# Gate weights of four heads multiplied in pieces inside the delta-rule pairs

## The chip, the cores and the metric

One core of one Trainium2 chip runs the whole program in one launch. The metric is the device time of that execution in microseconds (us), the median of several runs. Engines are named as in the profile: PE (TensorE) with its weight loads PEld, DVE (VectorE), ACT (ScalarE), POOL (GpSimd), and SP, which issues the DMAs.

## The reference, cut to what matters

A step of a 4-layer decoder trunk on 256 prompt positions and 8 samples of 8 positions, 320 columns in all, model width 1024. Layer 3 mixes tokens with a gated DeltaNet of 8 heads of 128 channels. Everything is fp32.

```python
qkv = silu(causal_dwconv(h @ w_qkv, conv_buf, w_conv))     # q, k, v; width-4 convolution
ab = h @ w_ab                                              # beta and log decay g of each head
lmat = strict_lower((k * beta) @ k.T * decay)              # chunks of 64 positions
u, w = solve(lmat + I, [v * beta, k * beta * exp(gc)])     # unit lower triangular
for each chunk:                                            # the state S goes from chunk to chunk
    v_new = u - w @ S
    o = (q * exp(g)) @ S + (q @ k.T * decay) @ v_new
    S = S * exp(g_last) + (k * exp(g_last - g)).T @ v_new
gate = silu(h @ w_g)                                       # one [128 x 320] tile per head
y = (rmsnorm(o) * gate) @ w_out
```

## The kernel before

**Units.** A weight matrix streams in units of 128 x 1024 fp32 (512 KB). SP loads a unit into one of four slots `raw`, ACT copies it rounded to fp32r into `whi` (`split_hi`, L1427), POOL subtracts and leaves the rest in `wlo` (`split_lo`, L610 and L612, a half each), and PE multiplies it with 8 row tiles of the normalised input. Each row tile takes three matmuls of 320 columns (high times high, high times low, low times high: L893 to L895), so a unit is 24 matmuls into one PSUM bank. A slot is free again when PE is through with its unit.

**The value and gate stage** (`d_vg`) has 16 units, in turn one of values and one of a gate for each of the 8 heads. DVE evicts a value unit into a padded buffer (L2341, L2342) and runs the width-4 convolution over it (L2345, L2348), ACT applies silu (L1783, L1784) and keeps the tail (L1786). A gate unit takes one eviction (L2370) and one silu (L1793) into the tile `GT`. Between units the engines also work out beta, the decays and the norms (`ab_*` semaphores), which SP stores to memory and reads back as broadcast rows: `rows_in` counts the three loads of a head (L466 to L468).

**The pairs** (`gdn_pair`) then take the heads two by two, `x` = 0 and 1. Four banks belong to each head of a pair. A pair has these parts:

- start: DVE scales keys by their norm (`keys`, L2417), POOL by beta (`scaled_keys`, L676); PE multiplies keys by keys (L1251) and keys by queries (L1257); DVE makes the matrix to be inverted (L2466 to L2470); PE turns keys, values and that matrix (L1189). Three matmuls of ones, whose result nobody reads, follow (`idle`, L1234).
- five levels of a block inversion. In each, PE runs `below` for both heads (L1278), ACT copies the result (L1878), PE runs `change` (L1289; in the last level L1298), DVE subtracts and transposes (L2487, L2491; in the last level L2499). The order is fixed: below 0, below 1, change 0, change 1.
- chunk steps: four chunks, PE (L1333 to L1373) and DVE (L2514 to L2542) in turn. L1333 is the batch of samples, matmuls of 16 columns. Beside them ACT and POOL prepare the next pair (L1897, L1844, L1832; L676, L704, L706), and POOL decays the sample states (L712) and spreads values over samples (L719).
- end: two more matmuls of ones, the state updates of the samples (L1379, L1380), DVE's additions to the states (L2549, L2550) and the product with the gate (L2554).

Pair 0 is written out, pairs 1 and 2 (and on PE pair 3) come from a loop. Pair 3 splits units 2 and 3 of the output projection where the others prepare the next pair. The names `Hh_spare`, `Hl_spare`, `M`, `sd`, `fsil` are lent buffers. No scheduler moves instructions: each engine runs its own list in the order written, and semaphores join the lists.

## Time and profile before

| what | us |
|---|---|
| median of 3 runs | 1556.9 (1553.49 to 1559.3) |
| the profiled execution | 1555.36 |
| its span, first to last instruction | 1553.6 |
| PE matmul busy in the span | 1523.0 (98%) |
| PE weight loads busy | 1481.7 (95%) |
| DVE, ACT, POOL busy | 799.6, 734.0, 1076.1 |

The span is the profiled execution without 1.8 us around it. Busy times are sums over the whole program; the change touches only the stretch from the value and gate stage to the end of the pairs, some 230 us of it. Matmuls overlap one another and their ends are modelled, so the row PE is always fuller than the engine.

### The profile page before, as it was taken

What the parts mean: (1) busy time and instruction counts of PE and PEld (TensorE: products, weight loads), DVE (VectorE), ACT (ScalarE), POOL (GpSimd) and SP (SyncE); (2) the same over time, 40 slices, a digit from 0 to 9 for tenths busy, and PEclk for the clock granted to TensorE, in tenths of its full rate; (3) what the DMA queues carried; (4) which work ended last, traced back from release to release, by engine and by line L of the source; (5) the groups of instructions that cost most, each with busy time, mean ns of one, the idle gap of its engine ahead of it and who ended that gap; (6) DMA issues with size and microseconds to landing.
All of it is one profiled execution on the core that took longest, in us unless ns stands there. A gap on an engine that the chain in (4) does not pass through costs nothing.

```text
span 1553.6 us, 32327 instructions
## 1 busy us (share of the span) xinstructions
PE 1523.0 (98%) x10258; PEld 1481.7 (95%) x10258; DVE 799.6 (51%) x1791; ACT 734.0 (47%) x1406; POOL 1076.1 (69%) x1041
## 2 busy tenths in 40 slices
PE   9999999999999999999999999999899999999998
PEld 9999999998999999888999999999888889999997
DVE  4555544017455313996555521666668766555401
ACT  6654444445444435566544433557534424444432
POOL 5568887764777678986777767666655556767674
PEclk9999999999999999999999999999999989999999
DMA  6344444552444655312565445544412215444453
GB/s 240 122 139 149 151 148 154 148 148 93 152 156 141 163 147 167 106 58 89 166 158 162 138 138 142 186 134 138 135 62 77 77 63 183 153 158 141 124 150 112
DMA packets 88111, 212.49 MB, mean 137 GB/s; under 512 B 25601, under 2 KB 33313, under 8 KB 88033
## 3 DMA queue, kind: packets, MB, share of 16 engines
q1 hardware_dynamic: 88032, 211.49, 44.2%
q8 instruction: 43, 0.70, 0.2%
q14 instruction: 36, 0.29, 0.1%
HBM read 201.80 MB, written 9.66 MB: 136 GB/s over the span
## 4 chain that ended last, share of the span: by engine, by line
PE 91%; DVE 5%; ACT 1%; issue 1%; DMA 1%; DVEq 0%; SPq 0%; POOL 0%; ACTq 0%; POOLq 0%
PE bank L893 26%; PE bank L895 26%; PE bank L894 26%; PE bank L1131 2%; PE bank L1289 1%; PE bank L1278 1%; PE bank L1333 1%; PE bank L1363 1%; PE bank L1184 1%; DMA fst<-in_d_st 1%; PE bank L1351 1%; PE bank L1354 0%; DVE bank L2263 0%; DVE Hh_spare L2468 0%; PE bank L1315 0%
## 5 line engine op out<-in xcount | busy, mean ns | idle before, releaser
L610 POOL TENSOR_TENSOR wlo<-raw,whi 128x512 fp32r<-128x512 f32 (+3 forms) x398 | 458.5, 1152 | 376.1 <-ACT whi L1427 338.6
L893 PE MATMUL bank<-Gh,whi 128*128 128x320 f32 x1912 | 596.6, 312 | 3.1 <-DVE M L2245 1.9
L895 PE MATMUL bank<-Gh,wlo 128*128 128x320 f32 x1912 | 591.1, 309 | 0.0
L894 PE MATMUL bank<-Gl,whi 128*128 128x320 f32 x1912 | 590.8, 309 | 0.0
L612 POOL TENSOR_TENSOR wlo<-raw,whi 128x512 fp32r<-128x512 f32 (+3 forms) x398 | 479.2, 1204 | 0.0
L1427 ACT ACTIVATE whi<-raw 128x1024 fp32r<-128x1024 f32 (+3 forms) x400 | 374.9, 954 | 52.9 <-PE bank L895 38.2
L893 PEld LDWEIGHTS bank<-Gh,whi 128*128 128x128 f32 x1912 | 359.3, 188 | 5.4 <-DVE M L2245 2.2
L894 PEld LDWEIGHTS bank<-Gl,whi 128*128 128x128 f32 x1912 | 359.3, 188 | 1.1
L895 PEld LDWEIGHTS bank<-Gh,wlo 128*128 128x128 f32 x1912 | 359.0, 188 | 0.0
L893 PE MATMUL bank<-Hh,whi 128*128 128x320 f32 x912 | 284.1, 311 | 4.0 <-DVE Hl L2204 2.5
L895 PE MATMUL bank<-Hh,wlo 128*128 128x320 f32 x912 | 282.3, 310 | 0.0
L894 PE MATMUL bank<-Hl,whi 128*128 128x320 f32 x912 | 282.2, 309 | 0.0
L1496 ACT ACTIVATE bank<-bank,par 128x336 f32<-128x336 f32 x88 | 45.3, 515 | 309.2 <-DVE bank L1985 309.2
L893 PEld LDWEIGHTS bank<-Hh,whi 128*128 128x128 f32 x912 | 171.5, 188 | 5.6 <-issue 3.6
L894 PEld LDWEIGHTS bank<-Hl,whi 128*128 128x128 f32 x912 | 171.6, 188 | 0.1
L895 PEld LDWEIGHTS bank<-Hh,wlo 128*128 128x128 f32 x912 | 171.6, 188 | 0.0
L2019 DVE TENSOR_TENSOR X<-bank,X 128x320 f32<-128x320 f32 (+1 forms) x32 | 15.7, 492 | 245.7 <-PE bank L895 245.7
L1975 DVE TENSOR_TENSOR fpad<-bank,R 128x256 f32<-128x256 f32 x88 | 37.4, 425 | 179.8 <-PE bank L895 179.6
L1462 ACT ACTIVATE Gh<-X,par 128x320 fp32r<-128x320 f32 (+1 forms) x48 | 27.0, 563 | 115.2 <-DVE X L2019 77.2
L2010 DVE TENSOR_TENSOR tmp<-bank,R 128x320 f32<-128x320 f32 x88 | 43.3, 492 | 55.1 <-PE bank L895 55.1
L1980 DVE TENSOR_SCALAR bank<-fpad,par 128x336 f32<-128x336 f32 x88 | 50.2, 571 | 21.9 <-DVE fpad L1976 21.6
L1982 DVE SCALAR_TENSOR_TENSOR bank<-fpad,par,bank 128x336 f32<-128x336 f32 x88 | 50.4, 573 | 12.4 <-DVE bank L1980 11.6
(392 smaller groups left out, 1812.0 us busy)
## 6 DMA issues: line engine op xcount, KB each, us to landing
raw<-in_f_up SPq DMA_DIRECT2D x176, 512.0 KB, 3.4
raw<-in_f_down SPq DMA_DIRECT2D x64, 384.0 KB, 3.2
raw<-in_f_down SPq DMA_DIRECT2D x64, 320.0 KB, 3.2
raw<-in_c_pw SPq DMA_DIRECT2D x24, 512.0 KB, 3.6
raw<-in_a_in SPq DMA_DIRECT2D x16, 512.0 KB, 4.1
raw<-in_d_qk SPq DMA_DIRECT2D x16, 512.0 KB, 3.8
raw<-in_d_vg SPq DMA_DIRECT2D x16, 512.0 KB, 3.6
raw<-in_a_out SPq DMA_DIRECT2D x8, 512.0 KB, 3.6
```

Source lines behind the costliest of these rows:

```text
L610: pool.tensor_tensor(wlo[k][:, 0:half], raw[k][:, 0:half], whi[k][:, 0:half].bitcast(F32), ALU.subtract).then_inc(half_ready, 1)
L612: pool.tensor_tensor(wlo[k][:, half:w], raw[k][:, half:w], whi[k][:, half:w].bitcast(F32), ALU.subtract).then_inc(lo_ready, 1)
L893: nc.tensor.matmul(dst, wh, h, start=start and n == 0, stop=False)
L894: nc.tensor.matmul(dst, wh, lo, start=False, stop=False)
L895: ins = nc.tensor.matmul(dst, wl, h, start=False, stop=stop and end and n == len(tiles) - 1)
L1131: ins = nc.tensor.matmul(mixb[i][:, 0:NT], diag[i][:, n * P:(n + 1) * P], windows(i, CONVW - PETAPS[m] + n), start=n == 0, stop=n == PETAP ...
L1427: nc.scalar.activation(whi[k][:, 0:w], raw[k][:, 0:w], ACT.Copy).then_inc(hi_ready, 1)
L1496: nc.scalar.activation(mixb[i][:, 0:FW - 2], mixb[i][:, 0:FW - 2], ACT.Silu, bias=col("f", j * 4 + (l * FT * 4 + 3))).then_inc(sil_ready, 1)
L1975: S.mark(vec.tensor_tensor(fp[:, 2:at], prompt(acc[2 * i]), prompt(R), ALU.mult))
L1980: S.mark(vec.tensor_scalar(ft[:, 0:n], fp[:, 0:n], col("f", w), None, ALU.mult))
L1982: S.mark(vec.scalar_tensor_tensor(out=ft[:, 0:n], in0=fp[:, 1:n + 1], scalar=col("f", w + 1), in1=ft[:, 0:n], op0=ALU.mult, op1=ALU.add))
L2010: vec.tensor_tensor(tmp[i][:, :], acc[2 * i + 1][:, 0:NT], R[:, :], ALU.mult).then_inc(evac, 1)
```

## The change

The gate units of heads 1, 3, 5 and 7 leave the stage, which keeps 12 units (value, gate, value for each two heads). Pair b multiplies the gate unit of head 2b + 1 itself: its 24 matmuls go to bank 5 in pieces of 2 or 3 between the products of the levels. The unit sits in slot 1; SP loads it early, and in the chunk steps of the pair before ACT makes its high part (`gate_high`) and POOL its low part (`gate_low`, one instruction over 1024 columns). DVE evicts the gate after the last level (`late_evac`), ACT applies silu in the chunk steps. Both fillers `idle` go. The keys by queries of head x = 1 move behind its turned keys and values have been read, into bank 6. Pair 3 splits units 1, 2 and 3 of the output projection, where it split 2 and 3. The beta and decay steps of the stage move to earlier units (after units 4, 5, 9 and 10, before 5, 7 and 11). `vp`, the levels' masked matrices and the row differences move to other buffers, since the weight slots are now in use in the pairs.

```diff
-                             [("d_ab", 4, 2 * P), ("d_qk", 16, 8 * P), ("d_vg", 16, 8 * P),
+                             [("d_ab", 4, 2 * P), ("d_qk", 16, 8 * P), ("d_vg", 12, 8 * P),
@@ SP
+            def load_gate(b):
+                if isinstance(b, int):
+                    sp.wait_ge(half_ready, START["d_vg", 3] + 10)
+                    sp.wait_ge(lo_ready, START["d_vg", 3] + 10)
...
+                else:
+                    sp.wait_ge(late_lo, b)
...
+                sp.dma_start(raw[1][:, 0:UNIT], src).then_inc(late_in, 16)
@@ POOL
+            def gate_low(b):
+                pool.wait_ge(late_hi, b + 1)
+                pool.tensor_tensor(wlo[1][:, :], raw[1][:, :], whi[1][:, :].bitcast(F32), ALU.subtract).then_inc(late_lo, 1)
...
                         pool.wait_ge(qt_ready, h + 1)
                         pool.tensor_tensor(deci[x], mincl[:, 0:NT], ndif[x], ALU.subtract).then_inc(diffi_ready, 1)
+                    gate_low(b + 1)
@@ PE
+                    def gate(a, z):
+                        if a == 0:
+                            pe.wait_ge(late_hi, b + 1)
+                            pe.wait_ge(late_lo, b + 1)
+                        for i in range(a, z):
+                            kt, part = i // 3, i % 3
+                            w = (whi[1], whi[1], wlo[1])[part][:, kt * P:(kt + 1) * P]
+                            ins = nc.tensor.matmul(bank[5][:, 0:NT], w, tile_of((Gh, Gl, Gh)[part], kt),
+                                                   start=i == 0, stop=i == 3 * KT - 1)
...
+                        if x == 1:
+                            gate(0, 3)
                         pe.wait_ge(tt_ready, h + 1)
                         turn(bank[4 * x], TT[x]).then_inc(t_turned, 1)
-                    idle(3, bank[5][:, TW:512])
...
                         for x in range(2):
                             below(lev, x)
+                        gate(*((3, 5), (7, 9), (12, 14), (17, 19), (22, 24))[lev])
                         for x in range(2):
+                            if lev == 0 and x == 1:
+                                pe.wait_ge(kv_scaled, b * 2 + 2)
+                                keys_by_queries(1, bank[6])
...
+                        if lev < 4:
+                            gate(*((5, 7), (9, 12), (14, 17), (19, 22))[lev])
...
-                    idle(2, bank[4][:, 0:P])
@@ ACT
+                def gate_high(b):
+                    act.wait_ge(late_in, b * 16 + 16)
...
+                    nc.scalar.activation(whi[1][:, :], raw[1][:, :], ACT.Copy).then_inc(late_hi, 1)
...
+                    def gated_late():
+                        act.wait_ge(late_evac, b + 1)
+                        separate(b)
+                        nc.scalar.activation(tile_of(GT, b * 2 + 1), tile_of(GT, b * 2 + 1), ACT.Silu).then_inc(gated, 1)
...
+                        gate_high(b + 1)
+                        gated_late()
                         values(b + 1)
                         decays(b + 1)
@@ DVE
+                        if lev == 4:
+                            dve.wait_ge(late_done, b + 1)
+                            vec.tensor_tensor(tile_of(GT, b * 2 + 1), bank[5][:, 0:NT], R[:, :], ALU.mult).then_inc(late_evac, 1)
```

PE in pair 0, from the turned values of head 1 to the first `change`: before.

```order
L1189 MATMUL bank<-ident,Hh_spare 128x128 [waits vf_ready]
L1189 MATMUL bank<-ident,Hh_spare 128x128 x2
L1189 MATMUL bank<-ident,Hl_spare 128x128 [waits tt_ready]
L1189 MATMUL bank<-ident,Hl_spare 128x128 x2
L1234 MATMUL bank<-ones 128x128 x3
L1278 MATMUL bank<-M,Gl_free 128x128 [waits lv_ready,t_ready]
L1278 MATMUL bank<-M,Gl_free 128x128 x2
L1278 MATMUL bank<-M,Gl_free 128x128 [waits lv_ready,t_ready]
L1278 MATMUL bank<-M,Gl_free 128x128 x2
L1289 MATMUL bank<-Hh_spare,Hl_spare 128x128 [waits vp_ready,b_ready]
```

The same place now (L1219 turns, L1277 is a piece of the gate, L1325 is `below`, L1336 `change`).

```order
L1277 MATMUL bank<-Gh,whi 128x320 [waits late_lo,late_hi]
L1277 MATMUL bank<-Gl,whi 128x320
L1277 MATMUL bank<-Gh,wlo 128x320
L1219 MATMUL bank<-ident,Hl_spare 128x128 [waits tt_ready]
L1219 MATMUL bank<-ident,Hl_spare 128x128 x2
L1325 MATMUL bank<-M,whi_free_51 128x128 [waits lv_ready,t_ready]
L1325 MATMUL bank<-M,whi_free_51 128x128 x2
L1325 MATMUL bank<-M,whi_free_52 128x128 [waits lv_ready,t_ready]
L1325 MATMUL bank<-M,whi_free_52 128x128 x2
L1277 MATMUL bank<-Gh,whi 128x320
L1277 MATMUL bank<-Gl,whi 128x320
L1336 MATMUL bank<-Hh_spare,Hl_spare 128x128 [waits vp_ready,b_ready]
```

The three matmuls of ones behind the turned matrix are gone; three matmuls of the gate stand ahead of it and two between `below` and `change`. Further levels look alike, with 2 or 3 matmuls behind each `below` and each `change`.

ACT at the end of the stage, the last two heads, before (L1427 splits, L1783 is the first silu of a value, L1793 that of a gate, L1844 starts the pairs).

```order
L1783 ACTIVATE VT<-bank 128x256 [waits conv_taps]
L1784 ACTIVATE VT<-bank 128x64
L1786 ACTIVATE fnew<-fpad 128x27
L1427 ACTIVATE whi<-raw 128x1024 [waits unit_done,raw_full0]
L1793 ACTIVATE GT<-GT 128x320 [waits psum_evacuated]
L1427 ACTIVATE whi<-raw 128x1024 [waits unit_done,raw_full1]
L1783 ACTIVATE VT<-bank 128x256 [waits conv_taps]
L1784 ACTIVATE VT<-bank 128x64
L1786 ACTIVATE fnew<-fpad 128x27
L1793 ACTIVATE GT<-GT 128x320 [waits psum_evacuated]
L1844 ACTIVATE Hh_spare<-VT 128x320 [waits qk_ready]
```

The same place now (L1484 splits, L1834 is the high part of the first late gate, L1854 a value, L1866 a gate, L1917 starts the pairs).

```order
L1484 ACTIVATE whi<-raw 128x1024 [waits unit_done,raw_full0]
L1854 ACTIVATE VT<-bank 128x256 [waits conv_taps]
L1855 ACTIVATE VT<-bank 128x64
L1857 ACTIVATE fnew<-fpad 128x27
L1834 ACTIVATE whi<-raw 128x1024 [waits unit_done,late_in]
L1866 ACTIVATE GT<-GT 128x320 [waits psum_evacuated]
L1854 ACTIVATE VT<-bank 128x256 [waits conv_taps]
L1855 ACTIVATE VT<-bank 128x64
L1857 ACTIVATE fnew<-fpad 128x27
L1917 ACTIVATE Hh_spare<-VT 128x320 [waits qk_ready]
```

The stage ended with a gate; it now ends with a value, whose convolution lies between PE's last matmul and the pairs.

POOL in the loop's chunk steps now (L705 is `gate_low`, L742 decays the sample states, L749 spreads values). Before, L706 was followed by L712 directly.

```order
L733 TENSOR_TENSOR fsil<-M,wlo_free_56 128x320 [waits nd_ready]
L735 TENSOR_TENSOR fpad<-M,wlo_free_56 128x320 [waits qt_ready]
L704 REGISTER_ALU
L705 TENSOR_TENSOR wlo<-raw,whi 128x1024 [waits late_hi]
L742 TENSOR_TENSOR M<-M,tmb 128x1024 [waits sv_done] x2
L749 TENSOR_TENSOR M<-ssq,M 128x512 [waits vns_ready] x2
```

A subtraction over 1024 columns now stands ahead of the two decays of the sample states.

## Rows read from the trace of the kernel before

**Rows 1.** Busy by stretch: stage, hand-over, pairs, levels, slow clock. Columns in line two.

```profile
core 0: us, PE busy (x) PEld busy (x) DVE busy (x) ACT busy (x) POOL busy (x), PEclk, DMA share, GB/s
1048.36:1108.41 60.05, 60.05 (x419) 59.98 (x419) 35.62 (x71) 39.84 (x76) 41.12 (x33) 1.00 0.50 147
1108.41:1120.75 12.34, 7.26 (x47) 6.44 (x44) 11.31 (x24) 7.45 (x19) 5.06 (x5) 0.86 0.24 84
1201.60:1242.32 40.72, 39.16 (x290) 35.05 (x290) 31.72 (x71) 17.45 (x43) 23.40 (x24) 0.96 0.27 87
1242.32:1280.81 38.49, 37.55 (x251) 33.88 (x252) 23.76 (x57) 10.46 (x25) 19.97 (x19) 0.87 0.18 63
1202.54:1217.08 14.54, 13.62 (x99) 11.66 (x97) 11.96 (x28) 5.07 (x14) 6.18 (x9) 1.00 0.48 154
1222.40:1225.81 3.41, 3.41 (x19) 3.41 (x17) 2.10 (x5) 2.90 (x7) 3.41 (x3) 0.50 0.00 0
1263.36:1273.60 10.24, 10.24 (x51) 10.23 (x50) 2.82 (x8) 0.47 (x1) 6.95 (x5) 0.50 0.00 0
```

**Rows 2.** Timeline: PE's last gate unit. Columns: start us, us, engine, instruction.

```profile
1104.89 0.31 PE L893 MATMUL bank<-Gh,whi 128*128 128x320 f32 x1
...
1108.41 0.71 PE L1227 MATMUL bank<-ident,M 128*128 128x128 f32 x5
```

**Rows 3.** Timeline: DVE and ACT, the last value and gate, start of the pairs.

```profile
1105.09 0.42 DVE L2341 TENSOR_TENSOR fpad<-bank,R 128x256 f32<-128x256 f32 x1 [2.94 <-PE bank L895]
...
1109.79 0.89 DVE L2417 TENSOR_TENSOR Hh_spare<-M,raw 128x320 f32<-128x320 f32 x2 [0.69 <-ACT GT L1793]
...
1108.14 0.39 ACT L1783 ACTIVATE VT<-bank 128x256 f32<-128x256 f32 x1 [4.17 <-DVE bank L2348]
...
1108.53 0.23 ACT L1786 ACTIVATE fnew<-fpad 128x27 f32<-128x27 f32 x1
```

**Rows 4.** Timeline: SP's stores and row loads; POOL's last split of the stage.

```profile
1096.09 0.32 SPq L435 DMA_DIRECT2D scr_n<-Hl_spare  x1
...
1100.39 0.33 SPq L466 DMA_DIRECT2D raw<-scr_n  x1
...
1102.66 0.43 SPq L468 DMA_DIRECT2D tmp<-scr_g  x1
...
1099.02 1.30 POOL L612 TENSOR_TENSOR wlo<-raw,whi 128x512 fp32r<-128x512 f32 x1
```

**Rows 5.** The page, part 5: weight loads of all units.

```profile
L893 PEld LDWEIGHTS bank<-Gh,whi 128*128 128x128 f32 x1912 | 359.3, 188 | 5.4 <-DVE M L2245 2.2
```

**Rows 6.** Timeline: weight loads of level 2 and the next, pair 2.

```profile
1212.19 0.97 PEld L1278 LDWEIGHTS bank<-M,Gl_free 128*128 128x128 f32 x8 [0.45 <-issue]
...
1213.38 0.97 PEld L1289 LDWEIGHTS bank<-Hh_spare,Hl_spare 128*128 128x128 f32 x8 [0.22 <-ACT Hh_spare L1878]
...
1214.67 0.97 PEld L1278 LDWEIGHTS bank<-M,Gf 128*128 128x128 f32 x8 [0.33 <-issue]
```

**Rows 7.** Timeline: weight loads of the turned matrix and the fillers, pair 2.

```profile
1201.60 0.31 PEld L1189 LDWEIGHTS bank<-ident,Hl_spare 128*128 128x128 f32 x3 [0.50 <-DVE Hl_spare L2470]
1201.88 0.75 PEld L1234 LDWEIGHTS bank<-ones 128*128 128x128 f32 x6
```

**Rows 8.** Timeline: DVE at level 2 and at the first chunk, pair 2.

```profile
1211.66 0.74 DVE L2487 TENSOR_TENSOR M<-M,bank 128x256 f32<-128x256 f32 x2
...
1219.17 0.28 DVE L2514 COPY Hl_spare<-bank 64x128 f32<-64x128 f32 x1 [0.61 <-PE bank L1317]
```

**Rows 9.** Timeline: POOL and DVE in the chunk steps of pairs 2 and 3.

```profile
1228.13 1.91 POOL L712 TENSOR_TENSOR M<-M,tmb 128x1024 f32<-128x1024 f32 x1 [2.17 <-PE bank L1334]
...
1231.02 1.04 POOL L719 TENSOR_TENSOR M<-ssq,M 128x512 f32<-128x512 f32 x1 [0.98 <-DVE ssq L2542]
...
1233.20 1.89 DVE L2422 TENSOR_TENSOR Hh_spare<-M,raw 128x320 f32<-128x320 f32 x2
...
1275.05 1.04 POOL L719 TENSOR_TENSOR M<-ssq,M 128x512 f32<-128x512 f32 x1 [2.49 <-DVE ssq L2542]
```

More of the change, by code:

```diff
@@ L157, in trunk_kernel @@
         raw = [sb(f"raw{i}", [P, UNIT]) for i in range(SLOTS)]
-        whi = [sb(f"whi{i}", [P, UNIT], F32R) for i in range(SLOTS)]
-        wlo = [sb(f"wlo{i}", [P, UNIT], F32R) for i in range(SLOTS)]
+        whi, whi_free, wlo, wlo_free = [], [], [], []
+        for name, part, free in (("whi", whi, whi_free), ("wlo", wlo, wlo_free)):
+            for i in range(SLOTS):
+                part.append(sb(f"{name}{i}", [P, UNIT], F32R))
+                free.append(nc.alloc_sbuf_tensor_at(f"{name}_free{i}", [P, UNIT], F32, offset=nc.sbuf_base - 4 * UNIT))
         X = sb("X", [P, KT * NT])
@@ L516, in _ @@
                 if name == "d_vg":
-                    with sp.Fori(0, 3) as b:
-                        for k in range(SLOTS):
-                            load(name, l, b, k)
-                    for k in range(SLOTS):
-                        load(name, l, 3, k)
+                    for j in range(n):
+                        load_vg(j)
+                    load("d_out", l, 0, 0)
+                    load_gate(0)
                     gdn_stores()
-                    load("d_out", l, 0, 0)
-                    load("d_out", l, 0, 1)
                     gdn_row_loads(0)
@@ L532, in _ @@
                 if name == "d_out":
+                    sp.wait_ge(late_lo, 4)
+                    load(name, l, 0, 1)
                     sp.wait_ge(kq_ready, HEADS)
@@ L696, in gdn_pair @@
                 if last:
-                    for k in range(2, 4):
+                    for k in range(1, 4):
                         split_lo(START["d_out", 3] + k, k, UNIT)
@@ L798, in _ @@
                 if name == "d_vg":
-                    with pool.Fori(0, 4) as b:
+                    with pool.Fori(0, 3) as b:
                         for k in range(4):
                             split_lo(b * 4 + (u0 + k), k, UNIT)
-                    for k in range(2):
-                        split_lo(START["d_out", 3] + k, k, UNIT)
+                    split_lo(START["d_out", 3], 0, UNIT)
+                    gate_low(0)
                     pool.wait_ge(gdn_in, 32)
@@ L1202, in _ @@
                 u0 = START["d_vg", 3]
-                for k in range(16):
+                for k in range(12):
                     in_unit(u0 + k, k % 4)
@@ L1216, in _ @@
                         ins.then_inc(ab_t, 1)
-                    if k == 11:
+                    if k == 9:
+                        pe.wait_ge(ab_v, RN_READY)
+                        turn(mixb[0], rnc, w=16).then_inc(ab_t, 1)
+                    if k == 10:
                         pe.wait_ge(ab_v, RW_READY)
@@ L1227, in _ @@
                     nc.tensor.transpose(dst, mlev[i], ident[:, :]).then_inc(masks_turned, 1)
-                pe.wait_ge(evac, u0 + 16)
+                pe.wait_ge(evac, u0 + 12)
                 pe.wait_ge(qk_ready, 24)
-                def idle(n, dst):
-                    for _ in range(n):
-                        nc.tensor.matmul(dst, ones[:, :], ones[:, :], start=True, stop=True)
                 def gdn_pair(b):
@@ L1252, in gdn_pair, with keys_by_queries @@
                         ins.then_inc(kk_done, 1)
-                    for x in range(2):
+                    def keys_by_queries(x, dst):
                         pe.wait_ge(kq_ready, b * 2 + (x + 1))
@@ L1256, in gdn_pair @@
                             w = (P, P, 64)[c]
-                            nc.tensor.matmul(T(bank[4 * x + 1], c, w), T(kh[x], c), T(qh[x], c, w), start=True, stop=True)
+                            nc.tensor.matmul(T(dst, c, w), T(kh[x], c), T(qh[x], c, w), start=True, stop=True)
+                    keys_by_keys(0)
+                    keys_by_queries(0, bank[1])
+                    keys_by_keys(1)
                     for x in range(2):
@@ L1786, in vg_half @@
                     nc.scalar.activation(new, tails(fpad[x], 3), ACT.Copy).then_inc(qk_tail, 1)
-                    if not (isinstance(b, int) and b == 3):
+                    if b < 3:
                         qk_history(n + 2, st + 6, x)
-                    if not last:
-                        split_hi(uv + 4, b * 16 + 16 * ((u0 + 2 * x + 4) // 4 + 1), (2 * x + 4) % 4, UNIT)
-                    act.wait_ge(evac, uv + 2)
-                    separate(h)
-                    nc.scalar.activation(tile_of(GT, h), tile_of(GT, h), ACT.Silu).then_inc(gated, 1)
+                    if x == 0:
+                        if b < 3:
+                            ring_hi(uv + 4)
+                        else:
+                            gate_high(0)
+                        act.wait_ge(evac, uv + 2)
+                        nc.scalar.activation(tile_of(GT, h), tile_of(GT, h), ACT.Silu).then_inc(gated, 1)
                 vg_half(0, 0)
```

84 lines of the change are left out of this document (56 added, 28 removed).

## The prediction

> **What bounds the kernel now.** I read four views, in this order. First the busy times by stretch [rows 1]. In the value and gate stage PE and its weight loads fill the stretch (59.98 of 60.05 us) while DVE, ACT and POOL have a third of it free: the stage is PE's, and what leaves its list there is saved. The hand-over to the pairs (12.34 us) has PE busy 7.26 and DVE 11.31: it is DVE's. A pair in steady state, start of the turned matrix to the same point a pair later, is 40.72 us with PE busy 39.16, so PE seems to fill it too.
>
> It doesn't. The weight loads are busy 35.05 us of the same pair, and 11.66 of the 14.54 us of the five levels [rows 1]: 2.88 us of gaps there. The Trainium skill ("Perfetto Trace Analysis", Identifying the Most-Contended Engine) says that matmul busy time is a poor measure of PE's headroom and that the weight loads' is the better one. By the matmul row a pair has 1.56 us free, and a moved unit would lengthen each pair by about 2 us (8 in all); by the loads' row it fits almost whole. The trace agrees with the rule as far as the next view goes.
>
> Then the timeline of one level. `below` starts at 1212.19, `change` at 1213.38, the next `below` at 1214.67, 8 loads each over 0.97 us [rows 6]. One load lasts 0.19 [rows 5], so they start (0.97 - 0.19) / 7 = 0.111 us apart, and 8 hold PE for 0.89. So PE waits some 0.30 us in the first half of a level and 0.40 in the second, both times for a chain through ACT or DVE. Last, the ends: PE's last unit begins at 1104.89 and ends at 1108.41, 3.52 us for 24 matmuls, 0.147 each [rows 2], and the first step of the pairs on DVE starts at 1109.79 [rows 3], 1.38 after PE's end.
>
> **The change part by part**, on the profiled execution (1555.36 us, span 1553.6).
>
> *Four units leave the stage:* 4 x 3.52 = **-14.1 us**. This needs the other engines to keep up. ACT does 39.84 us in 60.05 and POOL 41.12 [rows 1]; a gate unit takes 1.3 + 1.3 us of POOL with it, about 1.1 + 0.5 of ACT and 0.5 of DVE, so POOL has some 31 and ACT some 33 us of work in 46. Walking the lists of the three engines through the 12 units, I find PE waiting nowhere. The nearest is the product behind unit 5 that needs ACT's copy of the turned decays: about 0.4 us to spare. A miss costs 0 to 1 us; I take 0.
>
> *The stage ends with a value.* Before, the value's convolution ran beside the last gate unit and only an eviction and a silu followed. Now DVE starts 0.20 us after PE's end (1105.09 against a unit's start at 1104.89), ACT's first silu comes 3.05 later (1108.14), and silus and tail take 0.62 to 1108.76 [rows 3]; with 0.2 of hand-over `keys` starts 4.1 us after PE's end and not 1.38: **+2.7 us**. Nothing covers it, since DVE waits for the tail (`qk_tail`) ahead of `keys`.
>
> *The row loads come later against the end.* SP's last store was issued at 1096.09 and the row loads at 1100.39, right when POOL's last split ended (1099.02 + 1.30 [rows 4]), so they waited for the split, and the stores take 4.3 us at most, 0 at least. Now the rows are stored when DVE has copied the norms after unit 9, about 5.5 us before PE's end; with 2.2 us for the stores (half of the bound) the row loads go out 3 us before it. The six issues span 2.3 us [rows 4]. If the last one lands 5 to 6 us after its issue, it is there 4 to 5 us after PE's end, just when the second `keys` wants it. Bounds 0 and +2.6; I take **+0.3**.
>
> *First splits and masks:* `gate_high(0)` and `gate_low(0)` stand on ACT and POOL ahead of the pairs; by my walk POOL is through 3 us after PE's end, a microsecond before `keys` frees it to work. 0.
>
> *The clock at the hand-over.* The granted clock is 0.86 on average over it [rows 1]: PE had stood nearly idle, and one stretch ran at 1.2 instead of 2.4 GHz, beside DVE's work and so for nothing. PE now stands idle 2.7 us longer and has six instructions fewer there (the keys by queries of head 1). If the low clock lasts into the levels once more, 3.41 us at half speed cost up to 1.7. I take **+0.8**.
>
> *The levels.* 21 of the 24 gate matmuls go behind `below` and `change`: 2 x 0.147 = 0.29 us into a gap of 0.30, 3 x 0.147 = 0.44 into one of 0.40. The three first ones (0.44) lie in PE's wait of 0.50 for the matrix of head 1, and the 6 filler instructions behind it go (6 x 0.111 = 0.67 [rows 7]), so level 0 starts 0.6 us earlier, and levels 0 and 1, of three blocks and with smaller gaps, give that back to the pieces and to the moved product (which is not added, only moved). At level 2 the chain is DVE's anyway: it takes its subtractions back to back at 1211.66, without idle ahead [rows 8], so neither a small lead nor a small lag of PE arrives beyond it. Bounds: at best each pair keeps the 0.6 (-0.6), at worst no piece finds a gap, 21 x 0.147 - 0.6 = +2.5 a pair. I take +0.1.
>
> *DVE's late eviction*, 0.49 us, stands ahead of `keys` and the first copies of the chunk steps. DVE had 0.61 us idle behind the first copy [rows 8]; the first state update comes 0.3 later, the second 0.1, and PE goes on with the latter: +0.1.
>
> *ACT and POOL in the chunk steps.* ACT gets a split, a table load and a silu (some 2.8 us with the load back); it has 23 of 40.7 us free. POOL gets 2.6 us (two halves of 1.3 [rows 4]) ahead of the decays of the states. It had 2.17 + 0.98 us idle between L706 and L719 [rows 9], so L719 still finds its input last. 0. *The fillers at the pair's end*: in pairs 0 to 2 DVE works at `queries` then (1233.20 to 1235.09 [rows 9]) and PE waits for nobody who waits for it. 0. **Four pairs: 4 x 0.2 = +0.8 us.**
>
> *Pair 3* gets a third split, 2.6 us on POOL and 1.1 on ACT behind a table load. POOL had 2.49 us idle ahead of L719 [rows 9], but in a pair with 10.24 us at the low clock. **+0.5**, bounds 0 and 3.
>
> Sum: -14.1 + 2.7 + 0.3 + 0.8 + 0.8 + 0.5 = -9.0, so 1546.4 for the profiled execution. The median before is 1.5 us above the latter (1556.9): **forecast 1548 us**.
>
> **The rivals.**
> *A. The gaps don't take the pieces.* Each chain of a level is closed, and head 1 runs right behind head 0; a piece that starts late pushes both. For it: the gap behind `below` is as long as its piece to 0.01 us, and a piece of 3 is 0.04 longer than the gap behind `change`. Against: 2.88 us of gaps in the levels. The upper bound, 4 x (2.5 - 0.1) = +9.6: 1557.6, no change.
> *B. The clock turns the sum round: slower.* The fillers kept PE at work where DVE sets the pace. Without them the 1.2 GHz of the chunk steps could last until the next pair's levels, 20 us instead of 3.4. The price stands in the trace: from the turned matrix to L719 pair 2 takes 29.4 us and pair 3 32.7 [rows 1, 7, 9], 3.3 us more for 10.24 - 3.41 = 6.8 us more at the low clock [rows 1], 0.49 for one. So 16.6 us more cost 8 a pair: three pairs 24, pair 3 some 3 beyond what it pays already: 1575. It decides from 9.0 / 3 = 3 us a pair on. For it: pair 3 did stay low for 10 us. Against it: it fell there, as in pair 2, within the chunk steps behind the batch of 16-column matmuls, not near a filler, and recovered in spite of low work. The Trainium skill ("TensorE: Matmul & The Clock Gate", HAM oscillation) says that PE's gaps between bursts make its clock fall back again and again, which speaks against taking fillers out; the two levels it names are those the rows show.
> *C. POOL is late for L719* by its whole 2.6 us in pairs 0 to 2: +7.8, 1556. Against it: 3.15 us of idle there.
> *D. The stage's end and the levels go as well as they can:* no wait for rows, no clock loss, each pair 0.3 shorter and not 0.2 longer: 1548 - 0.3 - 0.8 - 2.0 = 1545.
>
> **How the numbers follow.** 0.5% (7.8 us) is about what a measurement of this kernel can tell from none, which puts the border to faster at 1549.1, a microsecond from the forecast. Forecast 0.58 (own range 1543 to 1552: 0.44 faster, 0.14 within), D 0.10 (faster), A 0.15 (within), C 0.09 (0.01 faster, 0.08 within), B 0.08 (0.07 slower, 0.01 within). Faster 0.55, within 0.38, slower 0.07. The range that holds 8 in 10 reaches down past D and up over C and A: 1542 to 1558.
>
> **What would show it.** The stage 14 us shorter, with no wait of PE in it; `keys` 4 us after PE's last unit; pairs of 40.7 to 41.1 us; weight loads busy some 37 us of a pair and not 35 (24 more, 10 fewer); each piece's `change` within 0.1 us of ACT's copy; L719's successor still released by DVE. I am wrong if pairs grow by over 1 us (then A or B, told apart by the granted clock), if rows hold `keys` back, or if DVE's chunk steps grow beside POOL's longer work.

## The result and the profile after

The changed kernel takes 1548.14 us (median of 7 runs, 1540.6 to 1552.9), the kernel before 1556.9 us (7 runs beside them, 1553.5 to 1559.3). The ratio is 0.9941, 95% interval 0.9925 to 0.9956: 9 us less, as forecast (1548). A second series gave 1547.71 us and 0.9936 (0.9919 to 0.9953).

The first profiled execution of the changed kernel is the slowest of its seven runs (1552.86 us, span 1551.1), so it shows only 2.5 us of the 9. The second (`after_again`, 1545.83 us, span 1544.1) is nearer to the median. The pieces of the three spans, in us; "matrix" is the start of head 1's matrix on DVE (L2470 before, L2554 now):

| piece | before | after | after_again |
|---|---|---|---|
| start to the stage | 1048.4 | 1051.1 | 1050.7 |
| stage to `keys` | 61.4 | 49.9 | 49.9 |
| `keys` to the matrix of pair 0 | 10.3 | 10.3 | 10.3 |
| three pairs, matrix to matrix | 121.6 | 125.9 | 122.6 |
| matrix of pair 3 to the output projection | 39.1 | 38.9 | 37.6 |
| the rest | 272.8 | 275.0 | 273.0 |

Row 2 holds what the change took, and rows 2 and 3 agree to 0.1 us in both profiles; rows 4 and 5 hold the pairs, which now do the moved work. Where the two profiles differ, low-clock stretches differ, also in the first row, whose code the change leaves alone. First the busy times by stretch of the first profile: the stage, the hand-over to the matrix, pairs 1 and 2, the levels of pair 2 (first `below` to the product behind the last subtraction), three stretches at the low clock, pair 3. The columns are those of [rows 1].

```profile
1051.06:1097.01 45.95, 45.95 (x323) 45.83 (x323) 30.08 (x62) 34.60 (x68) 27.85 (x22) 1.00 0.39 123
1097.01:1111.30 14.29, 7.62 (x39) 7.01 (x37) 13.08 (x27) 6.62 (x16) 8.02 (x8) 0.69 0.47 174
1151.98:1193.22 41.24, 39.76 (x305) 36.80 (x304) 31.92 (x71) 20.08 (x47) 25.66 (x25) 0.96 0.27 100
1193.22:1237.20 43.98, 42.90 (x305) 39.97 (x304) 31.92 (x71) 20.09 (x47) 25.69 (x25) 0.88 0.28 92
1194.11:1209.36 15.25, 15.18 (x127) 14.72 (x125) 12.74 (x30) 5.41 (x14) 6.85 (x9) 1.00 0.57 187
1102.50:1112.74 10.24, 8.35 (x38) 7.94 (x39) 10.10 (x23) 5.05 (x13) 4.83 (x6) 0.50 0.33 113
1215.14:1225.38 10.24, 10.24 (x50) 10.14 (x49) 2.57 (x9) 5.09 (x11) 7.28 (x5) 0.50 0.00 0
1269.75:1279.99 10.24, 9.35 (x25) 6.04 (x26) 6.64 (x12) 1.23 (x3) 3.46 (x4) 0.50 0.47 152
1237.20:1276.11 38.91, 35.85 (x268) 31.91 (x268) 25.49 (x62) 14.36 (x29) 21.86 (x21) 0.92 0.24 86
```

The stage is 45.95 us instead of 60.05 and PE is busy in all of it. In the levels the weight loads are now busy 14.72 of 15.25 us, before 11.66 of 14.54 [rows 1]: 0.53 us of gaps are left of 2.88. The levels are 0.71 us longer, but begin 0.67 us earlier (0.89 us behind the matrix of head 1 instead of 1.56), so they end as they did. Pair 2 took 43.98 us, with 10.24 us at 1.2 GHz in it.

The end of the stage, on DVE, to compare with [rows 3]:

```profile
1097.21 0.43 DVE L2424 TENSOR_TENSOR fpad<-bank,R 128x256 f32<-128x256 f32 x1 [3.05 <-PE bank L925]
...
1098.41 1.81 DVE L2431 SCALAR_TENSOR_TENSOR bank<-fpad,par,bank 128x344 f32<-128x344 f32 x3
1100.96 0.90 DVE L2501 TENSOR_TENSOR Hh_spare<-M,raw 128x320 f32<-128x320 f32 x2 [0.74 <-ACT fnew L1857]
```

`keys` starts 3.95 us behind PE's last unit (1097.01), 2.57 later than before (1.38). It waited for ACT's tail, not for rows.

Level 3 on the weight loads, pair 2 (L1325 is `below`, L1336 `change`, L1277 a piece of the gate). [rows 6] has the same level: the subtractions of level 2 [rows 8] stand ahead of its first `below`, so its rows are levels 3 and 4, though they are headed level 2.

```profile
1204.42 0.97 PEld L1325 LDWEIGHTS bank<-M,wlo_free 128*128 128x128 f32 x8
1205.31 0.19 PEld L1277 LDWEIGHTS bank<-Gh,wlo 128*128 128x128 f32 x1
1205.42 0.19 PEld L1277 LDWEIGHTS bank<-Gh,whi 128*128 128x128 f32 x1
1205.61 0.97 PEld L1336 LDWEIGHTS bank<-Hh_spare,Hl_spare 128*128 128x128 f32 x8
1206.50 0.19 PEld L1277 LDWEIGHTS bank<-Gl,whi 128*128 128x128 f32 x1
1206.61 0.19 PEld L1277 LDWEIGHTS bank<-Gh,wlo 128*128 128x128 f32 x1
1206.76 0.19 PEld L1277 LDWEIGHTS bank<-Gh,whi 128*128 128x128 f32 x1
1206.91 1.00 PEld L1325 LDWEIGHTS bank<-M,wlo_free 128*128 128x128 f32 x8
```

From `below` to `change` it is 1.19 us and on to the next `below` 1.30; before, 1.19 and 1.29. So this level pays nothing for its five matmuls of the gate. What they cost is paid in levels 0 and 1. The starts of DVE's subtractions of head 1 in pair 2 show it, in us behind the matrix. Two experiments from below stand beside them, one without the pieces and one with the fillers back:

| level | before | changed | no_pieces | fillers_back |
|---|---|---|---|---|
| 0 | 5.21 | 5.08 | 4.86 | 5.51 |
| 1 | 8.37 | 8.37 | 8.02 | 8.80 |
| 2 | 11.00 | 10.99 | 10.65 | 11.43 |
| 3 | 13.59 | 13.59 | 13.24 | 14.01 |
| 4 | 16.07 | 16.11 | 15.72 | 16.53 |

The pieces cost 0.22 us up to level 0 and 0.35 up to level 1, and from there on the distance hardly grows.

Pair 3, first POOL's last split and what follows it, then PE:

```profile
1264.59 1.26 POOL L636 TENSOR_TENSOR wlo<-raw,whi 128x512 fp32r<-128x512 f32 x1
1265.82 3.77 POOL L742 TENSOR_TENSOR M<-M,tmb 128x1024 f32<-128x1024 f32 x2
1269.55 2.03 POOL L749 TENSOR_TENSOR M<-ssq,M 128x512 f32<-128x512 f32 x2
```

```profile
1267.77 0.39 PE L1431 MATMUL bank<-ftap,ssq 128*128 128x64 f32 x2
1270.64 1.22 PE L1436 MATMUL bank<-M,Hh_spare 32*128 32x512 f32 x1 [2.48 <-POOL M L749]
```

POOL runs without a pause from its splits into L749, and PE waits 2.48 us for it. Before, DVE released L749's counterpart here [rows 9]. While PE waited the clock fell, for 10.24 us, and the output projection began at 1.2 GHz: its first unit took 5.42 us instead of 3.64, which is 1.8 of the 2.2 us that "the rest" is longer.

### The profile page after: what moved, and what is told of

It reads as the page before. It is cut to its first block, busy times and chain, and to the rows that moved or that the text cites. A ratio compares the mean times of both kernels' runs of the same rounds, so it can differ in the third digit from the quotient of the medians.

```text
span 1551.1 us, 32225 instructions
## 1 busy us (share of the span) xinstructions
PE 1518.2 (98%) x10218; PEld 1480.4 (95%) x10218; DVE 796.6 (51%) x1791; ACT 741.1 (48%) x1412; POOL 1073.9 (69%) x1037
## 4 chain that ended last, share of the span: by engine, by line
PE 90%; DVE 5%; issue 2%; POOL 2%; ACT 1%; DMA 0%; DVEq 0%; POOLq 0%; ACTq 0%
PE bank L923 26%; PE bank L925 26%; PE bank L924 26%; PE bank L1161 2%; PE bank L1325 1%; PE bank L1336 1%; PE bank L1391 1%; PE bank L1277 1%; PE bank L1214 1%; DVE bank L2346 0%; DVE Hh_spare L2552 0%; PE bank L1421 0%; DVE ssq L2038 0%; PE bank L1436 0%; POOL wlo L634 0%
## 5 line engine op out<-in xcount | busy, mean ns | idle before, releaser
L634 POOL TENSOR_TENSOR wlo<-raw,whi 128x512 fp32r<-128x512 f32 (+3 forms) x394 | 452.2, 1148 | 382.4 <-ACT whi L1484 345.0
L923 PE MATMUL bank<-Gh,whi 128*128 128x320 f32 x1880 | 587.8, 313 | 3.1 <-DVE M L2328 1.9
L925 PE MATMUL bank<-Gh,wlo 128*128 128x320 f32 x1880 | 582.4, 310 | 0.0
L924 PE MATMUL bank<-Gl,whi 128*128 128x320 f32 x1880 | 582.2, 310 | 0.0
L636 POOL TENSOR_TENSOR wlo<-raw,whi 128x512 fp32r<-128x512 f32 (+3 forms) x394 | 473.1, 1201 | 0.0
L1484 ACT ACTIVATE whi<-raw 128x1024 fp32r<-128x1024 f32 (+3 forms) x396 | 370.4, 953 | 55.7 <-PE bank L925 42.4
L923 PEld LDWEIGHTS bank<-Gh,whi 128*128 128x128 f32 x1880 | 354.2, 188 | 5.4 <-DVE M L2328 2.2
L924 PEld LDWEIGHTS bank<-Gl,whi 128*128 128x128 f32 x1880 | 354.2, 188 | 1.1
L925 PEld LDWEIGHTS bank<-Gh,wlo 128*128 128x128 f32 x1880 | 354.1, 188 | 0.0
```

What stands on the lines that cost most here:

```text
L634: pool.tensor_tensor(wlo[k][:, 0:half], raw[k][:, 0:half], whi[k][:, 0:half].bitcast(F32), ALU.subtract).then_inc(half_ready, 1)
L636: pool.tensor_tensor(wlo[k][:, half:w], raw[k][:, half:w], whi[k][:, half:w].bitcast(F32), ALU.subtract).then_inc(lo_ready, 1)
L923: nc.tensor.matmul(dst, wh, h, start=start and n == 0, stop=False)
L924: nc.tensor.matmul(dst, wh, lo, start=False, stop=False)
L925: ins = nc.tensor.matmul(dst, wl, h, start=False, stop=stop and end and n == len(tiles) - 1)
L1484: nc.scalar.activation(whi[k][:, 0:w], raw[k][:, 0:w], ACT.Copy).then_inc(hi_ready, 1)
```

## The experiments

All were timed in five rounds beside the kernel before, whose median was 1558.9, 1557.7 and 1556.2 us in the three series. A ratio is to it. The profile gives a second measure: a pair that happened to hold no low-clock stretch is the same to 0.02 us in kernels whose pairs are the same, so it shows tenths of a microsecond that the times can't.

**after_again**: no edit. 

> The changed kernel once more, for its interval and for a second profile. Theory: what took the 9 us is in the code, so the stage of values and gates is again 46 us long, keys come 3.9 us after TensorE's last unit, and pair 3's L1436 waits 2.5 us for GpSimd's L749; what differs between two profiles of it is where the stretches at the low clock fall (three of 10.24 us in the first profile). 1548 us, profiled execution anywhere from 1540 to 1553. Rival: the three long low stretches belong to the new order of work; then the second profile has them at the same three places.

1547.71 us, ratio 0.9936 (0.9919 to 0.9953). The low clock lay elsewhere: at the hand-over (13.65 us), 6.83 in pair 1, 3.41 twice in pair 3, none in pair 2. So both profiles have a long stretch at the hand-over and one behind pair 3's wait (10.24 and 3.41 us); elsewhere the stretches have no fixed place. Pair 2, undisturbed, is 39.62 us:

```profile
1193.88:1233.50 39.62, 38.14 (x305) 35.15 (x304) 31.93 (x72) 20.12 (x47) 25.64 (x25) 1.00 0.30 103
```

**no_pieces**: 22 of the 24 terms of a late gate are left out.

```diff
-                        for i in range(a, z):
+                        for i in range(max(a, 22), z):
...
-                                                   start=i == 0, stop=i == 3 * KT - 1)
+                                                   start=i == 22, stop=i == 3 * KT - 1)
```

> Of the 24 matmuls of a gate unit of an odd head only the last two are run in a pair, so the gates of the odd heads are left without 22 of 24 terms; loads, splits, eviction and silu stay. Theory (the gaps of the levels take the pieces, 0.05 us a pair lost): at most 1 us faster than the changed kernel, 1547, and the levels from turned T to the turned last change 15.5 us long as with them; weight loads 32.5 instead of 36.8 us of a pair. Rival A (the gaps do not take them, up to 2.5 us a pair): 1538 to 1542. A third possibility: TensorE with less to do falls to the low clock more often and the time rises.

1545.71 us, ratio 0.9924 (0.9900 to 0.9947), 2 us less than with all pieces, with intervals that overlap. The undisturbed pair says it more sharply:

```profile
1189.03:1228.26 39.23, 36.59 (x282) 32.50 (x282) 31.83 (x71) 20.09 (x47) 25.64 (x25) 1.00 0.30 104
```

39.23 against 39.62 us: 22 matmuls, 3.2 us of PE's time, cost 0.39 us a pair, all of it in levels 0 and 1 (the table above). The theory's 0.05 was too small. Rival A's 2.5 is refuted.

**one_block**: the unit unsplit.

```diff
-                            gate(0, 3)
+                            gate(0, 24)
...
-                        gate(*((3, 5), (7, 9), (12, 14), (17, 19), (22, 24))[lev])
...
-                        if lev < 4:
-                            gate(*((5, 7), (9, 12), (14, 17), (19, 22))[lev])
```

> All 24 matmuls of the gate unit in one block where the first piece of three stood (behind head 1's turned values, ahead of the turned T). Theory: a unit is 3.52 us and the wait there takes some 0.5 to 1.5 us of it, so each pair gets 2 to 3 us longer, four pairs 8 to 12: 1556 to 1560, what the change took is gone again. Rival: the time of the levels is set by VectorE alone, which has other work in that time; then the block costs under 1 us a pair, 1548 to 1551, and splitting the unit was needless.

1551.85 us (12 runs), ratio 0.9964 (0.9950 to 0.9979), which only touches the changed kernel's interval of the same series (up to 0.9953). Between theory and rival: +4.1 us, about half of what I expected. An undisturbed pair is 1.9 us longer:

```profile
1149.01:1190.52 41.51, 39.89 (x306) 35.81 (x305) 31.82 (x72) 20.10 (x47) 25.65 (x25) 1.00 0.28 99
```

Level 0 starts 3.24 us behind the matrix instead of 0.89, and the levels, now without pieces, win back 0.46. So splitting the unit is worth 1.9 us of a pair in steady state. Four such pairs would be 7.6 us, and the times show 4.1. Pair 0 doesn't explain it: it took 39.89 us without a low stretch against 39.22 in late_split, which had 2.74 us of low clock in its levels, so it lost more than the 0.7 between them. The rest is low clock (3.41 us in the first three pairs here, 10.9 and 18.4 in the two profiles of the changed kernel) or chance.

**fillers_back**: both groups of fillers in again.

```diff
+                    idle(3, bank[1][:, TW:512])
...
+                    idle(2, bank[4][:, 0:P])
```

The three stand behind the turned matrix of head 1, the two ahead of the wait for L749.

> The two groups of filler matmuls that the change took out are put back: three of 128 columns behind the turned T of head 1, two at the end of the chunk steps. Theory: they kept no clock up and stood in waits of TensorE, so nothing changes, 1547 to 1549.5. Rival B: without them the low clock lasts longer behind the chunk steps; then this kernel has fewer or shorter stretches at the low clock in the pairs than the changed kernel (24 us in its three first pairs), and is 2 to 6 us faster.

1547.55 us (12 runs), ratio 0.9937 (0.9918 to 0.9956): no change. Its undisturbed pair is 0.54 us longer:

```profile
1151.27:1191.43 40.16, 38.85 (x315) 36.19 (x314) 32.02 (x72) 20.11 (x47) 25.64 (x25) 1.00 0.30 103
```

The three first fillers stood on the path: `below` of level 0 starts 0.95 us behind the turn with them, 0.28 without, and 0.42 of it are left at the last subtraction; the rest of the 0.54 is the end's two (end_fillers has an undisturbed pair of 39.73, 0.12 more than without). Theory said nothing changes; in fact a loss of 2 us over four pairs was made up, which may be the clock (4.9 us low in the three first pairs, against 18.4 and 10.9 in the two profiles without fillers; the 24 of the expectations is too high).

**end_fillers**: only `idle(2, ...)` ahead of the wait for L749. 

> Only the two filler matmuls at the end of the chunk steps are put back. With both groups put back the levels became 0.43 us longer in each pair (the three fillers at the pair's start), the three first pairs showed 4.9 us at the low clock against 17 to 24 us without fillers, and the time was the same. Theory: the fillers at the end are what keeps the clock, and they cost under 0.2 us a pair; then the low clock in the pairs is short again without the 0.43: 1545 to 1546.5. Rival 1: the three at the start keep it; then low stretches as in the changed kernel, 1547 to 1549. Rival 2: fillers have no part in where the low clock falls, and its length in one profile is chance: 1547 to 1549 as well, with a profile of any length.

1544.41 us, ratio 0.9914 (0.9896 to 0.9932), apparently 3 us faster. But its pair 2 held 6.83 us at the low clock, and see `late_end` and `best`.

**late_split**: the third split of pair 3 behind L749.

```diff
-                    for k in range(1, 4):
+                    for k in range(1, 3):
                         split_lo(START["d_out", 3] + k, k, UNIT)
...
                     gdn_pair(3, True)
+                    split_lo(START["d_out", 3] + 3, 3, UNIT)
                     head_lo(6)
```

> The third split of the output projection's weights (unit 3) goes on GpSimd behind the last pair's L749 instead of ahead of its decays of the states. Theory: in pair 3 GpSimd, not VectorE, is the last that L749 needs (it starts 32.35 us behind the turned matrix's source against 29.1 in an undisturbed pair 2), so this takes 1.9 us off pair 3: L1436 at 31.5 instead of 33.4 us, and the time falls by 2 us to 1545.7 or so; if the wait there also lowered the clock behind it, by up to 4. Rival: VectorE's and ScalarE's work behind it sets the start of the output projection, or that projection now waits for unit 3's lower part; then 1547 to 1548 as with the changed kernel.

1541.09 us, ratio 0.9908 (0.9886 to 0.9929): 4.4 to 5.1 us less than the changed kernel by the ratios, 7 by the medians, so more than the theory's 2 and a little beyond its "up to 4"; the intervals touch. POOL's L749 starts 29.90 us behind the matrix of pair 3 instead of 32.35 and PE's product 30.99 instead of 33.43. Pair 3 up to the output projection:

```profile
1232.42:1266.39 33.97, 33.34 (x269) 30.83 (x269) 23.94 (x60) 14.14 (x29) 19.83 (x20) 1.00 0.25 87
```

33.97 us at full clock, against 38.91 and 37.62: 2.45 us of the wait are gone, and with it the low clock behind it. In the changed kernel both profiles had one there, as had all other kernels with the third split ahead (fillers_back, end_fillers, gate_last, no_pieces, one_block, one_gate); in the five with the split moved back, where PE waits 0.05 us or less, there was none at that place. The other eight have 3.4 to 10.2 us low there, behind waits of 0.9 to 2.5 us.

**gate_last**: the last three units as value, value, gate.

```diff
-t["d_vg"][j // 3 * 4 + j % 3, :, :]
+t["d_vg"][14 if j == 10 else 13 if j == 11 else j // 3 * 4 + j % 3, :, :]
```

with ACT's and DVE's lists of the last two heads in the same order. 

> The stage's last three units in the order value 6, value 7, gate 6 instead of value 6, gate 6, value 7. Theory: the convolution of value 7 then runs beside the last gate unit, and keys start 1.4 us after TensorE's last unit instead of 3.8 to 3.95: 2.4 us faster, 1545.3. Rival: the row loads, of which the last lands 4 us after TensorE's end, hold the second keys back; then the gain is at most 1 us, or none.

1546.51 us, ratio 0.9922 (0.9904 to 0.9940): 1.2 to 1.6 us less than the changed kernel by the medians, 2.2 to 3.0 by the ratios, with intervals that overlap, so the time doesn't tell theory (2.4) from rival (1). The trace does: `keys` starts 1.38 us behind PE's last unit again, 2.57 earlier, but from `keys` to the matrix it is now 11.85 us and not 10.34. That leaves 1.06, the rival's size, but mostly not for its reason. DVE, then POOL:

```profile
1097.71 1.77 DVE L2504 TENSOR_TENSOR Hh_spare<-M,raw 128x320 f32<-128x320 f32 x1 [0.69 <-ACT GT L1868]
1099.63 1.14 DVE L2504 TENSOR_TENSOR Hh_spare<-M,raw 128x320 f32<-128x320 f32 x1 [0.15 <-DMA tmp<-scr_g]
```

```profile
1096.78 2.35 POOL L705 TENSOR_TENSOR wlo<-raw,whi 128x1024 fp32r<-128x1024 f32 x1
```

The rows held the second `keys` for 0.15 us. The first took 1.77 us where one takes 0.49 otherwise, and ended 0.35 us after POOL's subtraction over 1024 columns; the second took 1.14 and ended 0.35 us after POOL's next product (1099.55, 0.87 us).

**both**: the two edits. 

> late_split and gate_last together. They lie 170 us apart and share no engine's wait, so their gains add: 4.4 us faster than the changed kernel by theory, 1543.3; by the rivals 1546 to 1548.

1543.56 us, ratio 0.9907 (0.9882 to 0.9933): the theory's number, but no faster than late_split alone (0.9908); its profile had 10.24 us at the low clock in pair 1, so the microsecond of gate_last can't be seen in the time.

**one_gate**: late gates neither loaded nor split from pair 1 on.

```diff
-                        load_gate(b)
...
-                    gate_low(b + 1)
...
-                        gate_high(b + 1)
```

> The gate units of pairs 1 to 3 are neither loaded nor split: each pair multiplies with the parts of head 1's gate, so the gates of heads 3, 5 and 7 are computed from the wrong weights; pieces, eviction and silu stay. Theory: ScalarE's 1.1 us and GpSimd's 2.4 us in the chunk steps, and 512 KB of load a pair, lie in time that nobody waits for: pairs of 39.6 us without a low stretch, as with the changed kernel, and 1547 to 1548.5. Rival C: GpSimd is late for L749, or slows VectorE beside it; then the pairs are 0.5 to 2.5 us shorter and the time is 1538 to 1545.

1547.17 us, ratio 0.9941 (0.9924 to 0.9958): theory. Its pair 1, undisturbed:

```profile
1146.93:1186.54 39.61, 38.13 (x305) 35.16 (x304) 31.91 (x71) 19.16 (x46) 23.40 (x24) 1.00 0.26 91
```

39.61 against 39.62. Rival C is refuted, though narrowly: with the split POOL comes to L749 without a pause, 29.11 us behind the matrix; without it, it waits 0.98 us for DVE and starts at 29.05.

**late_end**: late_split and end_fillers. 

> late_split with the two filler matmuls at the end of the chunk steps. late_split took 2.4 us off the wait of L1436 in pair 3, and the low clock that had followed it did not come: 1541.1. Theory: the end's fillers cost 0.12 us a pair and take a little of the low clock away, so 1538 to 1541. Rival: the 3 us that end_fillers was faster than the changed kernel were chance, since its pair 2 still had 6.8 us at the low clock; then 1541 to 1543.

1543.89 us, ratio 0.9914 (0.9893 to 0.9936): the rival, and a little above it. The fillers at the end bring nothing here; each of pairs 1 to 3 had its 3.41 us at the low clock, 21 us behind the matrix, as in the kernel before.

**split0_late**: both, and the split of the projection's unit 0 moved to the end of pair 0.

```diff
-                    split_lo(START["d_out", 3], 0, UNIT)
                     gate_low(0)
...
                 if not (isinstance(b, int) and b == 0):
                     head_lo(b * 2 - 2)
+                else:
+                    split_lo(START["d_out", 3], 0, UNIT)
```

> Both, with one more move: GpSimd's split of the output projection's unit 0 goes from the hand-over to the end of pair 0. In gate_last the first keys took 1.77 us beside GpSimd's L705, against 0.48 where it had ended, so 1.5 of the 2.57 us won at the stage's end were lost again. Theory: with the split gone from there L705 ends 2.3 us earlier or nearly, keys take 0.5 to 0.6 us, and from keys to the last matrix of head 1 (L2554 of the changed kernel) it is 10.6 instead of 11.8 us; 1.2 us less than both, 1541 to 1542.5. Rival: the rows of head 1 land no earlier, so the second keys wait for them and the gain is under 0.5 us.

1539.68 us, ratio 0.9900 (0.9877 to 0.9922), the lowest of all. The hand-over is as the rival said: from `keys` to the matrix 11.67 us, 0.18 less than in gate_last.

```profile
1097.73 0.75 DVE L2506 TENSOR_TENSOR Hh_spare<-M,raw 128x320 f32<-128x320 f32 x1 [0.69 <-ACT GT L1870]
1100.14 0.49 DVE L2506 TENSOR_TENSOR Hh_spare<-M,raw 128x320 f32<-128x320 f32 x1 [1.66 <-DMA tmp<-scr_g]
```

```profile
1095.76 2.37 POOL L705 TENSOR_TENSOR wlo<-raw,whi 128x1024 fp32r<-128x1024 f32 x1 [5.14 <-ACT whi L1836]
```

The first `keys` is nearly free of POOL (and again ends 0.35 us after L705), but the second now waits 1.66 us for the rows of head 1. L705 started only 1.0 us earlier, since it waits for ACT. So the move is worth 0.2 us at the hand-over. It costs more at its new place. POOL at the end of pair 0, here and in late_split:

```profile
1140.92 1.52 POOL L634 TENSOR_TENSOR wlo<-raw,whi 128x512 fp32r<-128x512 f32 x1
1142.40 1.53 POOL L636 TENSOR_TENSOR wlo<-raw,whi 128x512 fp32r<-128x512 f32 x1
1143.88 1.69 POOL L713 TENSOR_TENSOR Hl_spare<-Hh_spare,tmb 128x320 f32<-128x320 f32 x2
```

```profile
1144.84 1.69 POOL L713 TENSOR_TENSOR Hl_spare<-Hh_spare,tmb 128x320 f32<-128x320 f32 x2 [0.82 <-DVE Hh_spare L2507]
```

L713 scales the keys of the next pair. It begins 17.91 us behind pair 0's last subtraction and not 15.81, and the next matrix comes 23.32 us behind it; in late_split, one_gate and `both` it is 22.5. So the moved split costs 0.80 us to win 0.18, and the kernel's lower time (3.9 us under `both` by the medians, 1.1 by the ratios, within the intervals) is clock or chance.

**best**: split0_late with the fillers at the end. 

> gate_last, late_split, the moved split of unit 0 and the fillers at the end of the chunk steps in one kernel. By theory the gains over the changed kernel add: 2.5 at the hand-over, 4 to 6 in pair 3, 0 to 3 of the clock: 1537 to 1541. By the rivals of its parts: 1541 to 1543. Both would beat the kernel before (1557) and the changed one (1548).

1542.02 us, ratio 0.9914 (0.9895 to 0.9932), short of the theory. With late_end that makes two pairs of kernels in which the end's fillers added 2 to 3 us and one in which they took 3; all three differences lie within their intervals. split0_late has the lowest time, 16.5 us under the kernel before by the medians and 5.6 to 8.5 under the changed one, but the times of late_split, `both` and split0_late can't be told apart; by the pieces of the traces `both` is the shortest, by 0.6 us under split0_late and 1.1 under late_split.

## Why the prediction was right, by its steps

The time and the mechanism were right: four units leave a stage that PE bounds, and the pairs take them into gaps of the weight loads. One term, pair 3, was wrong in size, and that it stayed hidden is luck. By step:

- *Four units leave the stage, -14.1*: measured -14.10, without a wait of PE. The list walk of ACT and POOL held.
- *The stage ends with a value, +2.7*: +2.57. gate_last shows what it could have been: about 1.1 of it can be had by the order of three units, since POOL or the rows take the rest.
- *Row loads, +0.3*: 0. SP issued the last store at 1091.30 and the first row load at 1092.76, 1.5 us later and not 2.2. The last row landed 4.0 us behind PE's end (1101.02), as estimated, and held nothing, since the second `keys` began at 1101.38. With `keys` early, rows hold it: 0.15 us in gate_last, 1.66 in split0_late.
- *First splits, 0*: right, and for the reason given: `gate_low(0)` ended at 1099.81, 2.8 us behind PE's end and 1.15 ahead of `keys`. What the prediction didn't see is what the order saved: with `keys` 2.6 us earlier (gate_last) the same subtraction makes the first one 1.3 us longer.
- *The clock at the hand-over, +0.8*: 0 up to the matrix, +0.9 and +1.9 behind it. It was 1.2 GHz for 10.24 us from 1102.50, and `keys` to the matrix is 10.34 us as before: DVE sets the pace there. But 1.44 us of the stretch lay in pair 0, and 4.05 in after_again. Before, none did. DVE's last subtractions of pair 0, before, after, after_again:

```profile
1135.80 0.42 DVE L2499 TENSOR_TENSOR Hl_spare<-Hl_spare,bank 128x256 f32<-128x256 f32 x1 [0.21 <-PE bank L1298]
```

```profile
1127.38 0.87 DVE L2583 TENSOR_TENSOR Hl_spare<-Hl_spare,bank 128x256 f32<-128x256 f32 x2 [0.97 <-PE bank L1348]
```

```profile
1128.05 0.87 DVE L2583 TENSOR_TENSOR Hl_spare<-Hl_spare,bank 128x256 f32<-128x256 f32 x2 [0.97 <-PE bank L1348]
```

  Head 1's (the second of each x2, 0.45 us in) begins 15.67, 16.53 and 17.60 us behind the matrix (1120.13, 1111.30, 1110.90). That the code itself makes pair 0 longer is unlikely: one_block had no low clock in pair 0, and its last subtraction there comes 0.5 us earlier than in its later pairs (17.50 against 18.00), before 0.4.
- *The levels, +0.1 a pair*: +0.04, and for the reason given: level 0 starts 0.67 us earlier (forecast 0.6), levels 0 and 1 give that back, and the later ones stay as they were. Measured one by one, the fillers' going gave 0.42 and the pieces took 0.39; the 0.07 that are missing to +0.04 fit the moved product, which no run isolates. The gaps that the prediction fills with the pieces are those of levels 3 and 4 (its "level 2" [rows 6] is level 3).
- *Late eviction, +0.1 a pair*: 0. late_end has the end's fillers, as the kernel before, and in its pair 1, as there, 3.41 us low from 21.1 us behind the matrix (21.2 before). The pair takes 40.77 us against 40.72 (`before` first):

```profile
1160.27:1200.99 40.72, 39.16 (x293) 35.05 (x292) 31.90 (x71) 17.53 (x43) 23.39 (x24) 0.96 0.25 88
```

```profile
1153.04:1193.81 40.77, 39.85 (x309) 37.15 (x308) 32.12 (x72) 20.09 (x47) 25.68 (x25) 0.96 0.29 101
```

  From the last subtraction of the levels to the next matrix it is 24.65 and 24.66 us, with the eviction in the second alone. Without the end's fillers such a pair is 40.63 us:

```profile
1188.89:1229.52 40.63, 39.55 (x305) 36.72 (x304) 32.02 (x71) 20.11 (x47) 25.69 (x25) 0.96 0.29 100
```

  That row is split0_late's pair 2, whose code in the loop is that of the changed kernel (low from 21.0 us). So levels, eviction and fillers together are -0.1 a pair and not +0.2.
- *ACT and POOL in the chunk steps, 0*: +0.01, so right (one_gate: 39.61 against 39.62), with a part of the reason wrong. Where no low clock stretches the pair, L749 is no longer released by DVE, which the prediction had named as a sign; POOL arrives 0.06 us later than DVE would let it. I took the 3.15 us of idle [rows 9] from a pair with a low stretch, which had made PE and DVE late and so POOL's slack large. At full clock, one_gate shows 1.19 + 0.98 = 2.17 us at the same place, 0.2 less than the split needs.
- *Pair 3, +0.5 (0 to 3)*: the term that was mis-sized. The same misreading made it small: POOL's 2.49 us of idle ahead of L719 [rows 9] came from 10.24 us of low clock. At full clock the third split costs 2.45 us of waiting and, in every profile, a stretch at 1.2 GHz behind it: late_split is 4 to 7 us faster. That it didn't spoil the forecast is luck: pair 3 of the kernel before had been slow as well, for its own low stretch, and 39.10 us there stand against 38.91 and 37.62.

Of the rivals, A is refuted by no_pieces and C by one_gate. B did not come: no low stretch reached from the chunk steps into the next levels; only the one of the hand-over reaches into levels, those of pair 0. Its price was about right: undisturbed 39.6, 41.24 us with 3.41 us low (25.6 us behind the matrix), 43.98 with 10.24, so 0.43 to 0.48 us for one; earlier in the chunk steps it is less (40.63 with 3.41, 0.30). Whether the fillers kept the clock up stays open. In the pairs 0 to 2 of the four profiles with fillers in the new order of work 4.9 to 9.5 us are low, in the nine without 3.4 to 18.5, and only the latter have stretches of 10.24; but the times do not follow. The rule on oscillation that the prediction cited (the Trainium skill, "TensorE: Matmul & The Clock Gate", HAM oscillation) would have fillers help; the runs neither show nor exclude it.

## What to carry to other kernels

Work of an engine-bound stage can go into the gaps of a later one, if it is cut to the size of the gaps: read the gaps from the weight loads, not from the matmuls, and expect some of the moved time back as cost (here 0.39 of 3.2 us, all of it in the two levels with small gaps), not none. Compare the same level before and after. Slack is to be read in a stretch at full clock: slack beside a low-clock stretch is lent by it. And behind such a move look at the ends, the last unit of the emptied stage and the last round of the filled one, where the steady state's cover is missing; here they held 1 us and 4 to 5 us. And a piece of work that is moved out of one wait is to be priced where it lands (split0_late: 0.18 us won, 0.80 lost).

## What the runs showed of the hardware

VectorE's product of two operands in SBUF did not end here while a GpSimd operation that read SBUF was under way. The same 320-column product took 0.49 us alone (split0_late, 1100.14), 1.77 us when it started 1.42 us before the end of GpSimd's L705 (gate_last) and 0.75 when it started 0.40 before it (split0_late), and ended 0.35 us behind it both times. The convolution, which reads one operand from a bank, ran beside L705 at its usual pace (1098.41, L705 from 1097.46 to 1099.81 in the first profile: 1.81 us for three, and one takes 0.58 beside GpSimd or alone). The Trainium skill ("SBUF — State Buffer", Who interferes with whom) says that a VectorE instruction with two SBUF inputs contends with GpSimd's reads, and one with at most one SBUF input doesn't. By that rule, the trace agrees in both halves.

How far runs of one kernel lie apart depends in part on where the low clock falls. Up to the stage, where all the kernels are the same, the fourteen profiles differ by 5.5 us: the stage begins at 1047.6 with 3.4 us at the low clock on the way (one_gate) and at 1053.1 with 13.7 (late_end). No single profile's span gives the price of an edit of 2 us; pairs without a low stretch did.
